# A two-layer backbone on one core: weight sums set between product sums in the second feed-forward, another bank choice in its first step, and another order of the first loads

## The reference

```python
for l in range(2):                       # 512 latent tokens x, 256 context tokens h, width 1024
    zx = modulate(rms_norm(x, norm1_g[l]), mx[0], mx[1])     # mx, mc: silu(c) @ w_mod[l] + b_mod[l]
    zc = modulate(rms_norm(h, norm1_g[l]), mc[0], mc[1])
    ...                                  # zx @ w_in, retention, windowed attention, chunk gating
    x = x + mx[2] * (concat(ret_x, att_x, cm_x) @ w_out[l])
    z = modulate(rms_norm(x, norm2_g[l]), mx[3], mx[4])
    x = x + mx[5] * ((silu(z @ w_gate[l]) * (z @ w_up[l])) @ w_down[l])   # hidden width 2816
    if l == 0:
        ...                              # the same for the context tokens
return rms_norm(x, final_norm_g)
```

## Time and profile before

| | us |
|---|---|
| median of 3 runs (1784.77 to 1786.43) | 1786.2 |
| the profiled execution's own time | 1788.14 |
| its span, of which the rows tell | 1786.4 |
| PE busy | 1629.4 |
| DVE, POOL, ACT busy | 824.1, 614.6, 589.2 |

### The profile page before, as it was taken

How to read it: one execution, slowest core, us unless ns; L and a number is a source line. 1 busy time by engine, 2 the same in 40 slices (tenths; PEclk the granted TensorE clock), 3 DMA queues, 4 the chain that set the end, 5 groups by cost and what they waited for, 6 DMA issues and landing times.

```text
span 1786.4 us, 25688 instructions
## 1 busy us (share of the span) xinstructions
PE 1629.4 (91%) x10030; PEld 1348.2 (75%) x10030; DVE 824.1 (46%) x1335; ACT 589.2 (33%) x1011; POOL 614.6 (34%) x331
## 2 busy tenths in 40 slices
PE   3799997879799999999999998998789799999997
PEld 2588774448688888888888887876457688988986
DVE  3642356642433123232223246437634676676675
ACT  4222227641341212121212116235533633433433
POOL 0822241012222323232323221244004376776771
PEclk8799997879799999999999998999789899999999
DMA  6555430000413332213332210141003232222221
GB/s 240 182 186 150 143 94 24 1 1 24 165 47 118 119 118 94 85 56 117 117 117 94 71 48 24 48 94 48 1 1 94 64 102 94 94 94 94 94 71 47
DMA packets 122197, 155.27 MB, mean 87 GB/s; under 512 B 20352, under 2 KB 89872, under 8 KB 122128
## 3 DMA queue, kind: packets, MB, share of 16 engines
q1 hardware_dynamic: 122128, 154.32, 26.9%
HBM read 152.21 MB, written 2.10 MB: 86 GB/s over the span
## 4 chain that ended last, share of the span: by engine, by line
PE 77%; DVE 11%; ACT 4%; issue 4%; SPq 2%; DMA 1%; DVEq 0%; POOL 0%; ACTq 0%; POOLq 0%
PE ps L1846 13%; PE ps L1847 12%; PE ps L1848 12%; PE ps L2157 4%; PE ps L2158 3%; PE ps L2159 3%; PE ps L2254 2%; PE ps L2256 2%; PE ps L2255 2%; PE ps L1771 2%; PE ps L2065 2%; PE ps L2269 2%; PE ps L2271 2%; PE ps L2043 2%; PE ps L2270 2%
## 5 line engine op out<-in xcount | busy, mean ns | idle before, releaser
L524 POOL TENSOR_TENSOR wl<-raw,wh 128x1024 fp32r<-128x1024 f32 (+1 forms) x182 | 363.8, 2009 | 735.0 <-ACT wh L648 734.8
L1846 PE MATMUL ps<-zh,wh 128*128 128x512 f32 x1248 | 435.5, 349 | 9.1 <-POOL zl L524 5.7
L1847 PE MATMUL ps<-zl,wh 128*128 128x512 f32 x1248 | 432.3, 346 | 0.0
L1848 PE MATMUL ps<-zh,wl 128*128 128x512 f32 x1248 | 428.6, 343 | 0.0
L1846 PEld LDWEIGHTS ps<-zh,wh 128*128 128x128 f32 x1248 | 236.2, 189 | 68.6 <-issue 29.0
L1848 PEld LDWEIGHTS ps<-zh,wl 128*128 128x128 f32 x1248 | 235.3, 189 | 31.1
L648 ACT ACTIVATE wh<-raw 128x1024 fp32r<-128x1024 f32 (+1 forms) x182 | 155.1, 869 | 313.2 <-PE ps L1848 231.8
L1847 PEld LDWEIGHTS ps<-zl,wh 128*128 128x128 f32 x1248 | 236.1, 189 | 28.3
L1704 DVE TENSOR_TENSOR hf<-gs,ps 128x512 f32<-128x512 f32 (+1 forms) x44 | 22.4, 550 | 269.6 <-ACT gs L1060 269.6
L524 POOL TENSOR_TENSOR wl_d<-raw_d,wh_d 128x1024 fp32r<-128x1024 f32 x42 | 100.2, 2406 | 117.7 <-ACT wh_d L648 117.7
L1723 DVE SCALAR_TENSOR_TENSOR xT<-ps,modcol,xT 128x512 f32<-128x512 f32 (+1 forms) x176 | 104.1, 616 | 63.2 <-PE ps L2159 61.9
(11 more groups left out here) (292 smaller groups left out, 2983.8 us busy)
## 6 DMA issues: line engine op xcount, KB each, us to landing
raw<-in_w_gate_dram SPq DMA_DIRECT2D x22, 1024.0 KB, 5.5
raw<-in_w_up_dram SPq DMA_DIRECT2D x22, 1024.0 KB, 6.5
raw_m<-in_w_mod_dram SPq DMA_DIRECT2D x22, 1024.0 KB, 5.0
raw_d<-in_w_down_dram SPq DMA_DIRECT2D x21, 1024.0 KB, 4.9
raw<-in_w_in_dram SPq DMA_DIRECT2D x14, 1024.0 KB, 5.4
raw<-in_w_mod_dram SPq DMA_DIRECT2D x11, 1024.0 KB, 5.7
raw_n<-in_w_mod_dram SPq DMA_DIRECT2D x9, 1024.0 KB, 5.1
raw<-in_w_out_dram SPq DMA_DIRECT2D x32, 256.0 KB, 4.2
```

The costliest lines, as they stand in the source:

```text
L524: nc.gpsimd.tensor_tensor(dst, src, hi.bitcast(F32), ALU.subtract).then_inc(sem(done), 1)
L1846: MM(dst, wt_h[:, h, w], zh[:, k, c0:c1], start=(k == 0), stop=False)
L1847: MM(dst, wt_h[:, h, w], zl[:, k, c0:c1], start=False, stop=False)
L1848: last = MM(dst, wt_l[:, h, w], zh[:, k, c0:c1], start=False, stop=(k == KC - 1))
```

## The change

It has five parts.

1. VectorE in steps 1 to 10 of the second feed-forward: the sums for the up weights stand one by one between the posts of the gate panel, those for the next gate weights go from the take-outs of the down projection to the up panel (S1, S2, S3) and to the start of the next gate panel (S4); the eight take-outs follow each other.
2. ScalarE: the copies `h_hi` stand between the roundings of the next gate weights, the first product of the next gate panel is copied out before the last `h_hi`, and the seventh rounding moves into the next gate panel. GpSimd: `lo_down` comes after the first remainder of the next gate weights instead of after the seventh.
3. Banks: the gate panels keep accumulator c in bank 1 instead of 5; the gate panel of step 1 has banks 7, 2, 5, 6, 2 for a to e, and the semaphore values follow.
4. Step 1: ScalarE copies its first product out right after the last rounding, ahead of the activation of step 0, and VectorE makes the first three up sums ahead of the gating of step 0.
5. The start: the ten small loads are issued by ScalarE after its first two activations; SP issues the first `w_in` panel after the seventh `w_mod` panel (number 6 from 0), then the eighth, the tables, and the eight `bsb` loads, which have a semaphore of their own, waited for only in `gate`.

```diff
+        W_BANK = [{"a": 7, "b": 2, "c": 1, "d": 4, "e": 3}, {"a": 1, "b": 2, "c": 5, "d": 4, "e": 3}]
+        W_BANK_1 = {"a": 7, "b": 2, "c": 5, "d": 6, "e": 2}
...
             for q in range(5, 8):
                 sp.wait_ge(sem("use_mod"), q - 2)
                 startup_panel(q)
+                if q == 6:
+                    sp.dma_start(raw[0][:, :].rearrange("p (k n) -> p k n", k=KC),
+                                 win_v[0][:, :, PANEL_COL["rv"]:PANEL_COL["rv"] + 256]).then_inc(sem("ld_in0"), 16)
...
-                lo_w(1, 0)
+                lo_w(1, 0, range(7))
                 lo_down(1, 0)
                 with pool.Fori(1, FSTEPS - 1) as s:
-                    lo_w(s, 1)
-                    lo_w(s + 1, 0)
+                    lo_w(s, 1, range(7))
+                    lo_w(s + 1, 0, range(1))
                     lo_down(1, s)
+                    lo_w(s + 1, 0, range(1, 7))
...
+                first_sum(1, 0)
-                for h in (1, 0):
+                for h in (0, 1):
                     nc.scalar.activation(gs1[:, h, :], ps[:, 3 * h, :], ACT.Silu).then_inc(sem("gs_rdy1"), 2)
...
-                def gate_panel(s):
+                def gate_panel(s, first=False):
+                    if not first:
+                        weight_sum(s, 0, "S4")
                     post(s, 0, 0)
+                    if not first:
+                        weight_sum(s, 1, "S1")
                     post(s, 0, 1)
...
+                    down(s - 1, range(KC))
...
+            for name in ("S1", "S2", "S3"):
+                weight_sum(1, 1, name)
...
-            pe.wait_ge(sem("ld_small"), 16 * 18)
+            pe.wait_ge(sem("ld_small"), 16 * 10)
```

More of the change, by code:

```diff
@@ L338, in _ @@
                 startup_panel(q)
[L339 to L349, removed]
+            for q in range(5, 8):
+                sp.wait_ge(sem("use_mod"), q - 2)
+                startup_panel(q)
+                if q == 6:
+                    sp.dma_start(raw[0][:, :].rearrange("p (k n) -> p k n", k=KC),
+                                 win_v[0][:, :, PANEL_COL["rv"]:PANEL_COL["rv"] + 256]).then_inc(sem("ld_in0"), 16)
+            for to, of, n in ((S_MASK, K_MASK, 1152), (S_DIST, K_DIST + 384, P), (S_RC, K_RC, 2 * SX)):
+                sp.dma_start(K[:, to:to + n], consts[:, of:of + n]).then_inc(sem("ld_tables"), 16)
             for l in range(DEPTH):
@@ L352, in _ @@
                     sp.dma_start(bsb[64 * (g % 2):64 * (g % 2) + 64, l, g // 2, :],
[L353 to L360, removed]
+                                 cm_b_s[l, g].partition_broadcast(64)).then_inc(sem("ld_bsb"), 16)
             def a_free(a, first=False):
@@ L772, in up_panel @@
                     if not last:
-                        for i in range(3):
-                            hi_w(s + 1, 0, i)
+                        hi_w(s + 1, 0, 0)
                     hi_down(1, s)
                     if not last:
-                        for i in range(3, 7):
-                            hi_w(s + 1, 0, i)
-                    for n in range(4):
-                        h_hi(s, n)
+                        hi_w(s + 1, 0, 1)
+                        hi_w(s + 1, 0, 2)
+                    h_hi(s, 0)
+                    if not last:
+                        hi_w(s + 1, 0, 3)
+                    h_hi(s, 1)
+                    if not last:
+                        hi_w(s + 1, 0, 4)
+                        hi_w(s + 1, 0, 5)
+                    h_hi(s, 2)
+                    if not last:
+                        first_sum(s + 1, 0)
+                    h_hi(s, 3)
                 for n, t in enumerate(("T3", "T1", "T2", "T4")):
@@ L798, in ffn_later @@
                 hi_down(1, 0, first=True)
-                gate_panel(1)
+                gate_panel(1, first=True)
                 up_panel(1)
@@ L1373, in gate_panel, with up_panel @@
                     post(s, 0, 4)
-                def down_panel(s, last=False):
-                    for i, name in enumerate(("S1", "S2", "S3", "S4")):
-                        down(s - 1, range(2 * i, 2 * i + 1))
-                        if not last:
-                            weight_sum(s + 1, 0, name)
-                        down(s - 1, range(2 * i + 1, 2 * i + 2))
-                def up_panel(s):
+                    down(s - 1, range(KC))
+                def up_panel(s, last=False):
+                    if not last:
+                        weight_sum(s + 1, 0, "S1")
                     post(s, 1, 0)
+                    if not last:
+                        weight_sum(s + 1, 0, "S2")
                     post(s, 1, 1)
@@ L1387, in up_panel @@
                     gated(s, 1)
+                    if not last:
+                        weight_sum(s + 1, 0, "S3")
                     h_lo(s, 0)
@@ L2235, in products @@
                         elif i == 1:
-                            if not first:
+                            if up and type(s) is int and s == 1:
+                                pe.wait_ge(sem("gs_rdy1"), 7)
+                            elif not first:
                                 pe.wait_ge(sem("po"), 5 * q - 4)
@@ L2266, in down_later @@
                             pe.wait_ge(sem("ev_d1"), KC * s + n)
+                        if start and n == 1:
+                            pe.wait_ge(sem("gs_rdy1"), 8)
                         dst = ps[:, (0, 6)[n % 2], :]
```

82 lines of the change are left out of this document (50 added, 32 removed).

## The result

The changed kernel takes 1762.2 us (median of 4 runs, 1757.2 to 1763.4) against 1786.3 for the kernel before (4 runs): ratio 0.9858, 95% interval 0.9834 to 0.9881. The forecast was 1760, within 1754 to 1769. The profiled execution took 1763.39 us, its span 1760.7, 25.7 less than before.

The account below looks back on a forecast made before the run. TensorE was taken as the bound nearly everywhere, so only its standstills count. Start 9.0, step 1 2.7 and later steps 15.2 sum to 26.9 us off the profiled 1788.14; from the median 1759.3, said as 1760, range 1754 to 1769.

Parts of the forecast that it names:

- Steps 2 to 10: Second feed-forward's later steps: removing TensorE's waits gains 15.2 us of 17.0 counted, bounds 8.0 to 17.0.
- The three waits: TensorE's jumps at gate products P3 and P6 and in the down chunks: 0.38, 1.04 and 0.50 us a step.
- P6: Gate panel product waiting for VectorE's post 2: 0.2 us a step expected to remain, bounds 0 to 1.0.
- Step 1: Second feed-forward's step 1: early copy `ew` removes a 3.77 us stand, next wait is for `loD1`; 2.7 us gained.
- my lower bound: In step 1: only 0.9 us gained if the 2.8 us stand lowers the clock again.
- The start: Up to TensorE's first projection: 10.5 us earlier, less 1.5 for x and ctx landing later, so 9.0; bounds 3.6 to 10.5.
- GpSimd's first remainder is next, and the gain stands: At the start: `w_in` remainder directly follows GpSimd's multiplications, its 2.0 us wait goes, and the 10.5 us reach the first projection.
- Between: From the first projection to gate P2 of step 1: 0 gain forecast.
- the end: Behind the last step: nothing changes, the 1.9 us stop before the last down projection stays; 0 forecast.
- P6's stop: Rival in the later steps: the stop stays near 1.0 us, giving 1766.5; chance 0.13.
- ScalarE was not held at all: Rival at the start: ScalarE is held while issuing the small loads, start gains 3.6, giving 1765; chance 0.15.
- GpSimd's remainders were not late: Slower rival: second remainder behind `lo_down` comes late each step, against 0.8 us of slack, giving 1801; chance 0.04.

Follow-up runs that it names:

- run with the later sums: Changed kernel with VectorE's sums S1, S2, S3 each one post later and S4 behind the fourth post: 1755.4 us, ratio to the kernel before 0.9854.
- run with the remainders behind: Changed kernel with GpSimd's two first `w_in` panel remainders held until VectorE's first part of `zl` is written: 1759.5 us (one run).
- run with one remainder more: Changed kernel with one unused GpSimd subtraction added after `lo_down` in steps 1 to 9: 1766.0 us, ratio to the kernel before 0.991.

## Why the prediction was right, and where it was not

- **Steps 2 to 10 (15.2 forecast, 15.4 measured).** The three waits go as worked out, but P6 keeps 0.44 us a step instead of 0.2, 2.2 us over nine. What covers it is a count that was too low. The run with the later sums keeps no such wait, and its step is 31.03: so the step of the earlier trace rows, 33.18, held 2.15 us, not 1.9, and the nine steps 19.0 (321.34 - 302.36), not 17.0. That 15.4 meets 15.2 is in part luck, as the two errors cancel. A step is 31.43 where I said 31.3. The mechanism, turns of sums and remainders, is in the earlier trace rows and in the rows after: 2.41 became 1.45. The Trainium skill (SBUF — State Buffer, Who interferes with whom) has that a VectorE instruction with two SBUF inputs contends with a GpSimd one that reads SBUF; here the sums take 0.68 to 1.46 us in steps 2 to 10 of the changed kernel, and the posts, with one input in PSUM, always 0.41 to 0.43.
- **Step 1 (2.7, measured 2.5).** The stop moved to `loD1` as said: 2.42 us, where I had "up to 3". The clock stayed up after it here and in the second trace (2.38). In six of the variants' traces the stop was 2.57 to 2.59 us and the clock fell after it, which costs 1.5 us more: the reason that I gave for my lower bound, and I had let it count for nothing in the 2.7.
- **The start (9.0, measured 7.2).** This term was mis-sized by 1.8. The gain as far as the norm's sum is 36.46 - 29.38 = 7.1, near what I had; ctx landed 1.7 late, where I charged 1.5. The 2.0 us of GpSimd's wait for ScalarE's rounding went too. The step of the prediction that failed is "GpSimd's first remainder is next, and the gain stands": I followed GpSimd's queue to its end and did not look at what its earlier remainder would now lie beside. Before, VectorE did its scaling while GpSimd waited for ScalarE; now GpSimd's remainders lie on it. The gains end at 53.61, with the first remainder (53.57), the first scaling at 56.16, behind the second one (55.87), and `zl` is written at 58.42. Against the run with the remainders behind, that is 3.6 us more for gains and scaling. Without the hold TensorE would have waited for the remainders alone, to 55.87, so I estimate the cost at 2.7 us. It is more than the 1.8 missing, mainly since the remainders themselves took 4.63 us instead of 5.36. The prediction named the exclusion in the loop and did not apply it 1,400 us earlier. The Trainium skill (SBUF — State Buffer, Who interferes with whom) says that VectorE's one-source operations in a two-port mode contend as well; the scaling (one tensor in SBUF) at 3.61 instead of 1.64 us agrees.
- **Between (0, measured 2.3) and the end (0, measured -1.6).** The first is not the change's, as far as the traces tell. The stretch between took 1345.6 to 1357.0 us over fourteen traces, 1350.3 and 1357.0 for the same kernel before, 1351.7 and 1354.7 for the changed one. Layer 0's attention, full of short stops, runs at different granted clocks, and so does layer 1's: in a stretch from its attention to gate P2 of step 1 the same 734 matmuls take 163.9 us at 0.86 in the changed kernel and 158.4 at 0.89 in the run with one remainder more. The busy times of 280 to 400 us (columns as in the earlier trace rows) of the changed kernel's second trace, and of the run with the later sums:

```profile
280.00:400.00 120.00, 92.24 (x614) 59.28 (x613) 67.64 (x146) 64.36 (x142) 7.67 (x7) 0.88 0.02 3
```

```profile
280.00:400.00 120.00, 93.97 (x595) 59.13 (x594) 66.24 (x144) 62.69 (x141) 7.60 (x6) 0.81 0.01 2
```

  Clock 0.88 with 614 matmuls in the window, and 0.81 with 595, in code that does not differ. At the end the changed kernel has the same stop of 1.9 us as before, and then the clock fell, which it did not before. This may be the change's own doing (see the last section):

```profile
1729.27 0.71 PE L2306 MATMUL ps<-hh,wh_d 128*128 128x512 f32 x1 [1.91 <-issue]
1729.78 0.63 PE L2307 MATMUL ps<-hl,wh_d 128*128 128x512 f32 x1
...
1732.76 0.40 PE L2308 MATMUL ps<-hh,wl_d 128*128 128x512 f32 x1
```

- **The sum (26.9, measured 25.7 in the span, 24.1 in the medians).** 25.1 of it are the three terms; the two other stretches nearly cancel here, which is luck. On another chip the changed kernel's median is 16.7 us below, its ratio 0.9896, so 17 to 24 us is what whole times say.
- **The rivals.** P6's stop stayed at 0.44, not 1.0; ScalarE was not held at all; GpSimd's remainders were not late, with some 0.5 us to spare. The second run of the changed kernel has the same steps (305.92) and start (58.74).

## What to carry to other kernels

Where two engines exclude each other, put their long operations so that each waits only for a short one of the other, and put the operation that TensorE waits for ahead of them, not behind: in this loop 2.41 us became 1.45, and one place further forward gave 0.44 us a step more. When a start gets faster, list what each engine now does at the same time as the others and not only what follows what: the second-order loss here (2.7 us) came from an overlap that had not been there. And compare traces by landmarks in the program: a term of 4 us can't be seen in whole times that carry 10 us of granted clock.

## What was not expected of the hardware

- A stop of 1.91 us before the last down projection left the clock up in some executions and lowered it in others: 6 to 8 matmuls of 512 columns at 0.43 us intervals in nine of fourteen traces, none in five, with the same instructions on both sides of the stop. It is not spread evenly. Of the ten traces with the new steps (waits of at most 0.8 us) nine show it, all but the one with step 1 copied late; of the four whose steps hold the old waits or the stops for `lo_down` none does. So the denser steps may bring on the 1.6 us lost at the end; no run here tests it. In step 1 the clock fell after all six stops of 2.57 to 2.59 us and after none of the four of 1.96 to 2.42; with `lo_down` last again it fell after one of 2.41 and stayed up after one of 3.15.
- ScalarE issued ten transfers in 4.7 us (3.42 to 8.16), none held for more than 0.73, while one of SyncE's took 4.50 (4.46 to 8.96); another of SyncE's took 9.38 just after. So what held SyncE there did not hold ScalarE. The Trainium skill (DMA: Bandwidth & Descriptors, Issuing engines are not separate DMA queues) says that only the time to issue is saved by a second issuer. The run with the small loads on SyncE agrees: the second issuer gained nothing over one queue in the right order.
- 0.6 MB of small loads beside the tokens cost the context 1.3 to 1.9 us of landing (13.73 to 14.06 in nine traces, 12.14 to 12.42 in the three with the old start); issued behind it on its own queue, at most 0.6 (12.48 and 12.75).
